# Eight chunks of the first block's modulation: from the tensor engine's row sums to GpSimd products and folds beside the choice of keys

## The chip, the cores and the metric

The kernel runs on one core of a Trainium2 chip. The metric is the device time of one execution in microseconds. Three runs of the kernel before took 4020.67, 4022.31 and 4030.84 us; their median, 4022.31 us, is the time to be compared.

## The reference, cut to what matters

The program computes two transformer blocks one after the other on 1024 tokens of width 1024, all in float32. The part that matters here is the first block's modulation and the choice of keys:

```python
c_act = jax.nn.silu(c)
mod = jnp.matmul(c_act, ada_w[l]) + ada_b[l]          # 1024 -> 6 * 1024
sh1, sc1, gt1, sh2, sc2, gt2 = [m[:, None, :] for m in jnp.split(mod, 6, axis=-1)]
h = rmsnorm(x, norm1_g[l]) * (1.0 + sc1) + sh1
proj = jnp.matmul(h, w_in[l])
...
score = jnp.einsum('bqh,bqhk->bqk', wi[:, start:end].astype(jnp.float32), jax.nn.relu(dots))
_, idx = lax.top_k(score, kk)                          # 256 keys of each query
```

`mod` is one row of 6144 numbers, made in twelve chunks of 512 columns. The first four chunks (sh1, sc1) are needed before anything else; the other eight (gt1, sh2, sc2, gt2) are needed only after the first block's attention.

## The kernel before, in words

The program is written in stages. A stage ends when all five engines have reached its end; then the next one starts. The change lies in one stage, `choose`, which runs from 210.5 to 690.5 us of the profiled execution. Three things run side by side in it.

**The choice of keys.** For the query tiles 2 to 7 (128 queries each; every key is kept for tiles 0 and 1) the scores are made in four pairs of heads per tile, 24 pairs in all. For each pair TensorE makes the products (`ch_s`, L590), ScalarE rectifies them into `ch_relu` (L621), and VectorE adds them, weighted, into `ch_score`: two instructions per pair, the first of a tile at L644 (tensor_scalar), the others at L647 (scalar_tensor_tensor, which reads `ch_relu` and `ch_score`, both in SBUF). I call such a pair of instructions a gather and number them 0 to 23. The choice itself is VectorE's: 32 rounds per tile of the eight largest (L662) and their replacement (L663), and one comparison that writes the mask (L666). After every eighth round of a tile comes one gather for the next tile. So gathers 4 to 23 lie between the rounds of tiles 2 to 6, and tile 7's rounds have none between them.

**The side work of the tensor engine.** A list of tasks (`side_work`) is dealt out to the 24 pairs by a table of costs: 8 small tasks for the logits of the forget gate (`log`), 56 tasks for seven further chunks of `w_in` times eight token tiles (`column`, L564, eight matmuls each), and 8 tasks for the modulation (`vector`). What is left after the last pair comes at the end. ScalarE copies each result out (L610), and for `log` and `column` its queue stores it (L612). ScalarE takes the rectifying and the copies in the order of the list, as TensorE does. TensorE may be two results ahead of the copies. ScalarE rectifies pair u only when gather u-2 is done (`used`).

**A vector task** takes 512 columns of `ada_w`, loaded as [128, 8, 512]. `row_sums` (L100) multiplies each of the eight slices with a broadcast column of silu(c) on a quarter of the array, which leaves four partial rows. ScalarE copies them to `ch_row` (L604). One task later `turn` calls `row_columns` (L108): four matmuls against `pick`, a vector with ones in the four rows that count, which sum the partial rows and turn them into a column of four blocks in `ch_mod`. VectorE adds the bias (L669) as its last instruction of the stage.

SyncE loads two chunks of `w_in` (into `aT`) and one of `ada_w` (into `space`) in the stage before, and then each next one when the last task that reads the buffer is done (`side_done`), in the order of the list.

```python
while left and time > 0:
    time -= cost[left[0][0]]
    share.append(left.pop(0))
```

Of the kernel before, what the change touches and what calls it, by code (L numbers as in the profile page):

```python
# [460 lines left out]
def side_work():  # L461
# [11 lines left out]
    tasks += [("vector", n, None) for n in range(sum(k == "vector" for k, _, _ in tasks), len(vectors))]  # L473
    tasks = logs + tasks
    cost = {"log": 1.6, "column": 6.9, "vector": 4.3}
# [30 lines left out]
def choose(nc, g, iqT, ikT, mask, hT, wi, space, aT):  # L506
# [3 lines left out]
    with stage(nc, g) as ctx:  # L510
# [10 lines left out]
        row = [sb(f"row{b}", [P, CH]) for b in range(2)]  # L521
        mod_ps = ctx.enter_context(nc.psum_tensor("ch_mod", [P, CH], F32))
# [4 lines left out]
        turned = g.sem("ch_turned")  # L527
# [3 lines left out]
        rows_before = [sum(k == "vector" for k, _, _ in tasks[:i]) for i in range(len(tasks) + 1)]  # L531
        outs_before = [sum(k != "vector" for k, _, _ in tasks[:i]) for i in range(len(tasks) + 1)]
# [4 lines left out]
        def _(sp):  # L537
            sp.dma_start(w_log[:, :, :], g.d["w_in"][0].rearrange("(k p) n -> p k n", p=P)[:, :, C_FLOG:C_FLOG + H]).then_inc(log_loaded, 16)
            for i, (kind, n, t) in enumerate(tasks):
                if kind == "column" and t == NT - 1 and n + 2 < len(columns):  # L540
                    sp.wait_ge(side_done, i + 1)
                    load_columns(nc, g, sp, w, n + 2)
                if kind == "vector" and n + 1 < len(vectors):
                    sp.wait_ge(side_done, i + 1)
                    load_vector(nc, g, sp, w_vector, n + 1)

        @block.tensor
        def _(pe):
            def side(i, kind, n, t):
# [3 lines left out]
                if kind == "vector":  # L553
                    pe.wait_ge(g.vector_loaded, 16 * (n + 1))
                    row_sums(nc, side_ps[i % 2], w_vector, g.cT, 0).then_inc(side_done, 1)
                else:
                    if kind == "log":
                        pe.wait_ge(log_loaded, 16)
                        by, width = w_log, H
                    else:  # L560
                        pe.wait_ge(g.columns_loaded[n % 2], 16 * (n // 2 + 1))
                        by, width = w[n % 2], CH
                    for k in range(KD):
                        last = nc.tensor.matmul(side_ps[i % 2][:, 0:width], hT[:, k, t * P:(t + 1) * P], by[:, k, 0:width], start=k == 0, stop=k == KD - 1)  # L564
                    last.then_inc(side_done, 1)

            def turn(i):

                if tasks[i][0] == "vector":
                    k = rows_before[i]  # L570
                    pe.wait_ge(side_copied, i + 1)
                    row_columns(nc, mod_ps[:, 4 * k:4 * k + 4], row[k % 2], g.pick).then_inc(turned, 1)

            def share(i, tasks):
                for kind, n, tile in tasks:
                    side(i, kind, n, tile)
                    if i >= 1:
                        turn(i - 1)
# [15 lines left out]
            turn(i - 1)  # L594

        @block.scalar
        def _(act):
            def side(i, kind, n, t):
                act.wait_ge(side_done, i + 1)
                if kind == "vector":  # L600
                    k = rows_before[i]
                    if k >= 2:
                        act.wait_ge(turned, k - 1)
                    nc.scalar.copy(row[k % 2][:, :], side_ps[i % 2][:, :]).then_inc(side_copied, 1)  # L604
                else:
                    k = outs_before[i]
                    c, width = (C_FLOG, H) if kind == "log" else (columns[n], CH)
                    if k >= OUTS:
                        act.wait_ge(stored[k % OUTS], 16 * (k // OUTS))
# [2774 lines left out]
```

## Time and profile before

| what | us |
|---|---|
| median of three runs | 4022.31 |
| the profiled execution | 4012.1 |
| its span, first to last instruction | 4009.9 |
| TensorE busy in the span | 3754.8 (94%) |
| VectorE busy | 1635.1 (41%) |
| ScalarE busy | 963.8 (24%) |
| GpSimd busy | 328.6 (8%) |
| the stage `choose` | 210.5 to 690.5 |

The profile shows one execution. It is 10.2 us shorter than the median of the unprofiled runs; the sums of the prediction are made inside the profiled execution and then set on the median. GpSimd has no instruction between 0.5 and 708 us, so none in this stage. The chain that ended last does not reach back to this stage: it starts at 3066 us, and since each stage waits for the one before, what the stage gains or loses should be read from its own end.

### The profile page before, as it was taken

To read this page: it belongs to the slowest core of one execution; us is meant where nothing else is said; L and a number is where in the kernel's file an instruction comes from. 1 tells how busy PE (TensorE), PEld (TensorE's weight loads), DVE (VectorE), ACT (ScalarE), POOL (GpSimd) and SP (SyncE) were. 2 spreads that over 40 slices of the span, in tenths; PEclk is the share of its full clock that TensorE was granted. 3 is DMA by queue.
4 is the path that set the end of the run, shared out by engine and by line. 5 is a ranking of instruction groups with operands and counts; after the bars stand their busy time and mean duration, and the time that the engine had idled before them with its cause. 6 is when DMAs were issued, how large, how long until landed. Compare 5 with 4: busy or idle time off the path is not lost. (4 is left out here: it accounts for less than half of the span.)

```text
span 4009.9 us, 46596 instructions
## 1 busy us (share of the span) xinstructions
PE 3754.8 (94%) x18356; PEld 1983.8 (49%) x18356; DVE 1635.1 (41%) x2790; ACT 963.8 (24%) x2001; POOL 328.6 (8%) x302
## 2 busy tenths in 40 slices
PE   6999999999899599999987999999898999999998
PEld 3554444555454244444444457876654444444443
DVE  2469996655232100000002334555453343343246
ACT  2311111544232112212213312222243311111001
POOL 0000000311210201010111111121000000000000
PEclk8979999999999699999996899999898999999999
DMA  4213231111424799898957212322113111111334
GB/s 170 74 38 116 97 116 55 55 59 38 124 87 170 254 344 336 330 342 329 343 202 278 93 67 81 106 81 85 53 35 111 45 42 42 42 42 45 126 111 154
DMA packets 294780, 533.33 MB, mean 133 GB/s; under 512 B 24708, under 2 KB 103828, under 8 KB 292286
## 3 DMA queue, kind: packets, MB, share of 16 engines
q1 hardware_dynamic: 272574, 472.17, 34.2%
q0 software_dynamic: 12720, 43.76, 2.8%
q10 hardware_dynamic: 9296, 14.75, 1.0%
q8 instruction: 134, 2.20, 0.2%
q14 instruction: 56, 0.46, 0.0%
HBM read 462.77 MB, written 67.85 MB: 132 GB/s over the span
## 5 line engine op out<-in xcount | busy, mean ns | idle before, releaser
L564 PE MATMUL ch_side<-aT,space 128*128 128x512 f32 x896 | 392.5, 596 | 0.0
L1679 DVE TENSOR_SCALAR ex_y<-ex_y,ex_entry 128x1024 f32<-128x1024 f32 x32 | 41.1, 1284 | 635.1 <-PE ex_y L1599 635.1
L564 PEld LDWEIGHTS ch_side<-aT,space 128*128 128x128 f32 x896 | 168.3, 190 | 215.3 <-issue 214.1
L2903 PE MATMUL en_bank<-en_h,en_up 128*128 128x512 f32 x528 | 233.8, 592 | 0.0
L1583 PE MATMUL ex_a<-ex_w,ex_xT 128*128 128x512 f32 x512 | 227.6, 598 | 6.2 <-ACT ex_xT L1650 6.2
L1599 PE MATMUL ex_y<-ex_w,ex_actT 128*128 128x512 f32 x512 | 225.1, 592 | 0.7 <-ACT ex_actT L1662 0.7
L1583 PE MATMUL ex_b<-ex_w,ex_xT 128*128 128x512 f32 x512 | 225.0, 592 | 0.0
L2065 PE MATMUL mx_duo<-mx_chunks,mx_region 128*128 128x512 f32 x384 | 181.1, 627 | 0.0
L662 DVE MAX8 ch_best<-ch_score 128x8 f32<-128x384 f32 (+5 forms) x192 | 171.6, 894 | 6.1
L663 DVE MATCH_REPLACE8 ch_score<-ch_best,ch_score 128x384 f32<-128x384 f32 (+5 forms) x192 | 168.0, 875 | 0.0
L2903 PEld LDWEIGHTS en_bank<-en_h,en_up 128*128 128x128 f32 x528 | 100.2, 190 | 125.8 <-issue 125.8
L1583 PEld LDWEIGHTS ex_a<-ex_w,ex_xT 128*128 128x128 f32 x512 | 98.1, 192 | 129.8 <-issue 129.8
L2903 PE MATMUL en_bank<-en_h,en_mixed_up 128*128 128x512 f32 x352 | 158.2, 592 | 0.0
L2012 PE MATMUL mx_duo<-mx_late 64*64 64x64 f32 (+1 forms) x3632 | 146.0, 226 | 6.7 <-DVE mx_late L2644 5.0
L1650 ACT ACTIVATE ex_xT<-ex_x,modT,ex_gain 128x128 f32<-128x128 f32 x264 | 95.6, 467 | 222.8 <-PE ex_x L1588 222.8
L1599 PEld LDWEIGHTS ex_y<-ex_w,ex_actT 128*128 128x128 f32 x512 | 94.8, 190 | 108.0 <-issue 107.1
L1583 PEld LDWEIGHTS ex_b<-ex_w,ex_xT 128*128 128x128 f32 x512 | 94.9, 190 | 107.6 <-issue 107.6
L2012 PEld LDWEIGHTS mx_duo<-mx_late 64*64 64x64 f32 (+1 forms) x3632 | 121.7, 136 | 34.9 <-issue 30.3
L2067 PE MATMUL mx_duo<-mx_chunks,mx_region 128*128 128x256 f32 x512 | 123.2, 395 | 5.0 <-DMA mx_chunks<-w_in 5.0
L610 ACT COPY ch_out<-ch_side 128x512 f32<-128x512 f32 (+1 forms) x64 | 34.1, 533 | 370.6 <-PE ch_side L564 370.6
L3198 DVE TENSOR_TENSOR en_region<-en_region,en_bank 128x512 f32<-128x512 f32 x88 | 58.4, 684 | 158.3 <-PE en_bank L2903 66.6
L2065 PEld LDWEIGHTS mx_duo<-mx_chunks,mx_region 128*128 128x128 f32 x384 | 75.1, 201 | 93.3 <-issue 91.7
(521 smaller groups left out, 5754.7 us busy)
## 6 DMA issues: line engine op xcount, KB each, us to landing
ex_w<-exp_w SPq DMA_DIRECT2D x96, 2048.0 KB, 13.6
en_up<-w_down SPq DMA_DIRECT2D x132, 256.0 KB, 3.6
mx_x<-proj_padded SPq DMA_DIRECT2D x96, 256.0 KB, 3.5
space<-ada_w SPq DMA_DIRECT2D x8, 2048.0 KB, 8.4
space<-w_ada SPq DMA_DIRECT2D x8, 2048.0 KB, 19.7
aT<-w_in SPq DMA_DIRECT2D x7, 2048.0 KB, 8.7
proj<-ch_out ACTq DMA_DIRECT2D x56, 256.0 KB, 2.0
en_up<-w_gate SPq DMA_DIRECT2D x22, 512.0 KB, 5.0
```

Source lines behind the costliest of these rows:

```text
L564: last = nc.tensor.matmul(side_ps[i % 2][:, 0:width], hT[:, k, t * P:(t + 1) * P], by[:, k, 0:width], start=k == 0, stop=k == KD - 1)
L662: chain(nc.vector.max(best[:, :], sc))
L663: chain(nc.vector.match_replace(sc, best[:, :], sc, CHOSEN))
L1583: last = nc.tensor.matmul(ps[:, :], xT[b][:, k, :], w13[b][:, s, k, :], start=k == 0, stop=k == KD - 1)
L1599: last = nc.tensor.matmul(y_ps[:, c:c + CH], actT[:, k, :], w2[b][:, k, c:c + CH], start=k == 0, stop=k == F // P - 1)
L1650: last = nc.scalar.activation(xT[b][:, k, :], x_ps[:, k, :], ACT.Identity, bias=shift[:, k:k + 1], scale=gain[:, k:k + 1])
L1679: nc.vector.tensor_scalar(y[b][:, :], y_ps[:, :], entry[b][:, 2:3].bitcast(F32), None, ALU.mult).then_inc(y_ready, 1)
L2012: mm = lambda out, a, b, start=True, stop=True: nc.tensor.matmul(out, a, b, start=start, stop=stop)
L2065: last = nc.tensor.matmul(ps[:, :], hT[:, k, t * P:(t + 1) * P], w_qkv[c][:, k, :], start=k == 0, stop=k == KD - 1)
L2067: last = nc.tensor.matmul(ps[:, 0:256], hT[:, k, t * P:(t + 1) * P], w_half[c][:, k, :], start=k == 0, stop=k == KD - 1)
L2903: last = nc.tensor.matmul(to[:, :], a[:, k, :], b[:, k, :], start=k == 0, stop=k == HK - 1)
L3198: TT(C[a][b], C[a][b], up_bank(i, m)[:, :], op).then_inc(joined, 1)
```

## The change

The eight vector tasks leave the list of the tensor engine's side work, and the cost of a column in the table goes from 6.9 to 7.1. GpSimd gets a program in this stage: for each chunk it multiplies the whole [128, 8, 512] by silu(c) in place, and folds it in three additions to one [128, 512] in `ch_row`, each instruction waiting for the one before (`weighed`). The tensor engine keeps the four small matmuls per chunk, now against a vector of 128 ones, since all 128 partitions hold a part of the sum. They stand behind the last of tasks 14, 21, 28, 35, 42, 49, 56 and 63. SyncE loads the next chunk when the third fold of the last one is done, at the same places of its list.

```diff
         for t in range(NT):
             tasks.append(("column", n, t))
-            if len(tasks) % 7 == 4 and vectors[len(tasks) // 7:]:
-                tasks.append(("vector", sum(k == "vector" for k, _, _ in tasks), None))
...
-    cost = {"log": 1.6, "column": 6.9, "vector": 4.3}
+    cost = {"log": 1.6, "column": 7.1}
...
+        turn_behind = {NT + 7 * n + 6: n for n in range(len(vectors))}
...
-                if kind == "vector" and n + 1 < len(vectors):
-                    sp.wait_ge(side_done, i + 1)
-                    load_vector(nc, g, sp, w_vector, n + 1)
+                if i in turn_behind and turn_behind[i] + 1 < len(vectors):
+                    sp.wait_ge(weighed, 4 * (turn_behind[i] + 1))
+                    load_vector(nc, g, sp, w_vector, turn_behind[i] + 1)
...
-                if kind == "vector":
-                    pe.wait_ge(g.vector_loaded, 16 * (n + 1))
-                    row_sums(nc, side_ps[i % 2], w_vector, g.cT, 0).then_inc(side_done, 1)
...
+            def turn(k):
+
+                pe.wait_ge(weighed, 4 * (k + 1))
+                if k == 0:
+                    pe.wait_ge(one_set, 1)
+                row_columns(nc, mod_ps[:, 4 * k:4 * k + 4], row[k % 2], one).then_inc(turned, 1)
...
-                    nc.scalar.copy(row[k % 2][:, :], side_ps[i % 2][:, :]).then_inc(side_copied, 1)
...
+        @block.gpsimd
+        def _(pool):
+            nc.gpsimd.memset(one[:, :], 1.0).then_inc(one_set, 1)
+            for n in range(len(vectors)):
+                pool.wait_ge(g.vector_loaded, 16 * (n + 1))
+                if n >= 2:
+                    pool.wait_ge(turned, n - 1)
+                TT = nc.gpsimd.tensor_tensor
+                TT(w_vector, w_vector, g.cT[:, 0:KD].unsqueeze(2).broadcast_to([P, KD, CH]), ALU.mult).then_inc(weighed, 1)
+                pool.wait_ge(weighed, 4 * n + 1)
+                TT(w_vector[:, 0:4, :], w_vector[:, 0:4, :], w_vector[:, 4:8, :], ALU.add).then_inc(weighed, 1)
+                pool.wait_ge(weighed, 4 * n + 2)
+                TT(w_vector[:, 0:2, :], w_vector[:, 0:2, :], w_vector[:, 2:4, :], ALU.add).then_inc(weighed, 1)
+                pool.wait_ge(weighed, 4 * n + 3)
+                TT(row[n % 2][:, :], w_vector[:, 0, :], w_vector[:, 1, :], ALU.add).then_inc(weighed, 1)
```

The table of costs deals the columns anew. TensorE at pairs 6 to 8 (the first rows with a modulation chunk), before:

```order
L590 MATMUL ch_s<-at_ikT,space 128x512 x2
L100 MATMUL ch_side<-space,cT 32x512 x8
L564 MATMUL ch_side<-aT,space 128x512 x8
L108 MATMUL ch_mod<-pick,ch_row 128x1 x4
L590 MATMUL ch_s<-at_ikT,space 128x512 x2
L564 MATMUL ch_side<-aT,space 128x512 x8
L590 MATMUL ch_s<-at_ikT,space 128x512 x2
```

and now:

```order
L583 MATMUL ch_s<-at_ikT,space 128x512 x2
L557 MATMUL ch_side<-aT,space 128x512 x8
L583 MATMUL ch_s<-at_ikT,space 128x512 x2
L557 MATMUL ch_side<-aT,space 128x512 x16
L108 MATMUL ch_mod<-ch_one,ch_row 128x1 x4
L583 MATMUL ch_s<-at_ikT,space 128x512 x2
```

The row sums (eight matmuls of 32 columns of the array) are gone, the four small matmuls stay, and pair 7 has two columns instead of one. TensorE's last rows of the stage, before:

```order
L564 MATMUL ch_side<-aT,space 128x512 x40
L100 MATMUL ch_side<-space,cT 32x512 x8
L564 MATMUL ch_side<-aT,space 128x512 x8
L108 MATMUL ch_mod<-pick,ch_row 128x1 x4
L564 MATMUL ch_side<-aT,space 128x512 x72
```

and now:

```order
L557 MATMUL ch_side<-aT,space 128x512 x48
L108 MATMUL ch_mod<-ch_one,ch_row 128x1 x4
L557 MATMUL ch_side<-aT,space 128x512 x56
L108 MATMUL ch_mod<-ch_one,ch_row 128x1 x4
```

Behind the last pair stood 15 columns and a row sum of these rows (two of the columns belong to the pair's own share); now there are 13 columns, and the last four small matmuls stand behind the last column. GpSimd has this for every chunk (the third here), with its waits:

```order
L624 TENSOR_TENSOR space<-space,cT 128x4096 [waits ch_turned,vector_loaded]
L626 TENSOR_TENSOR space<-space 128x2048 [waits ch_weighed]
L628 TENSOR_TENSOR space<-space 128x1024 [waits ch_weighed]
L630 TENSOR_TENSOR ch_row<-space 128x512 [waits ch_weighed]
```

and SyncE's queue, which loads for it, has now:

```order
L535 DMA ch_w_log<-w_in 128x8x8
L500 DMA space<-ada_w 128x8x512 [waits ch_weighed]
L494 DMA aT<-w_in 128x8x512 [waits ch_side_done]
L500 DMA space<-ada_w 128x8x512 [waits ch_weighed]
L494 DMA aT<-w_in 128x8x512 [waits ch_side_done]
L500 DMA space<-ada_w 128x8x512 [waits ch_weighed]
```

The first `ada_w` load of the stage waits for no task of TensorE any more, and each later one but the last stands directly behind a load of `w_in` in the same queue.

## Rows read from the trace of the kernel before

**Rows 1.** Busy time by stretch (us, busy us and count of each engine, PEclk, DMA share, GB/s)
```profile
665.00:690.00 25.00, 22.29 (x52) 9.50 (x51) 0.00 (x0) 2.34 (x4) 0.00 (x0) 1.00 0.11 42
```

**Rows 2.** Groups by line, 205 to 692 us, VectorE
```profile
L647 DVE SCALAR_TENSOR_TENSOR ch_score<-ch_relu,at_wi,ch_score 128x384 f32<-128x384 f32 (+5 forms) x42 | 40.0, 951 | 38.2 <-ACT ch_relu L621 22.2 <-issue 12.5 <-DVE ch_score L663 0.7
```

**Rows 3.** Timeline of PE, one row sum and its turn (start us, us, what)
```profile
277.82 1.92 PE L100 MATMUL ch_side<-space,cT 128*32 128x512 f32 x16
...
279.67 7.13 PE L564 MATMUL ch_side<-aT,space 128*128 128x512 f32 x16
...
286.64 0.95 PE L108 MATMUL ch_mod<-pick,ch_row 128*128 128x1 f32 x8
```

**Rows 4.** Timeline, end of the stage and start of the next
```profile
664.79 0.19 DVE L669 TENSOR_TENSOR modT<-ch_mod,biasT 128x32 f32<-128x32 f32 x1
...
687.33 0.58 ACT L610 COPY ch_out<-ch_side 128x512 f32<-128x512 f32 x1 [6.28 <-PE ch_side L564]
...
690.49 0.37 SPq L749 DMA_DIRECT2D space<-proj  x1
```

**Rows 5.** Groups by line and form, GpSimd, whole program
```profile
L778 POOL TENSOR_TENSOR space<-space,ad_q_stat 128x1024 f32<-128x1024 f32 x8 | 14.9, 1899 | 19.1 <-DVE ad_q_stat L1024 19.1
...
L1334 POOL TENSOR_TENSOR space<-space,jn_gate_bias 128x2048 f32<-128x2048 f32 x8 | 36.1, 4509 | 100.3 <-DMA space<-proj 100.3
...
L2459 POOL TENSOR_TENSOR mx_early<-mx_early 128x1024 f32<-128x1024 f32 x8 | 19.2, 2397 | 60.9 <-DMA mx_early<-moe_y 60.9
```

**Rows 6.** One line's instructions: duration ns min/median/max, first and last start
```profile
L1387 DVE TENSOR_TENSOR jn_merged<-space x16: 691/693/5855, 1032.5 to 1242.5; 128x512 f32<-128x512 f32 x16
...
L1384 DVE TENSOR_TENSOR space<-space,jn_bank x16: 675/686/689, 1031.2 to 1241.2; 128x512 f32<-128x512 f32 x16
...
L2588 DVE TENSOR_REDUCE mx_pstat<-mx_psq x16: 685/686/687, 2244.4 to 2810.3; 128x8 f32<-128x512 f32 x16
```

**Rows 7.** Timeline of the joining stage, GpSimd and VectorE
```profile
1084.40 4.51 POOL L1334 TENSOR_TENSOR space<-space,jn_gate_bias 128x2048 f32<-128x2048 f32 x1 [6.85 <-DMA space<-proj]
...
1087.45 2.02 DVE L1387 TENSOR_TENSOR jn_merged<-space 128x512 f32<-128x512 f32 x1
```

**Rows 8.** Timeline of the mixing stage, GpSimd and VectorE
```profile
2534.05 1.49 POOL L2482 TENSOR_TENSOR mx_early<-mx_qkv,mx_tab 128x512 f32<-128x512 f32 x1
...
2534.57 1.52 DVE L2612 TENSOR_TENSOR mx_early<-mx_qkv,mx_tab 128x512 f32<-128x512 f32 x1
...
2535.51 1.49 POOL L2485 TENSOR_TENSOR mx_kd<-mx_qkv,mx_tab 128x512 f32<-128x512 f32 x1
```

**Rows 9.** Timeline of SyncE's queue; DMA issues, 240 to 692 us
```profile
310.96 0.37 SPq L497 DMA_DIRECT2D aT<-w_in  x1
...
space<-ada_w SPq DMA_DIRECT2D x7, 2048.0 KB, 8.0
```

**Rows 10.** Timeline of VectorE, instructions that add scores
```profile
238.90 1.34 DVE L647 SCALAR_TENSOR_TENSOR ch_score<-ch_relu,at_wi,ch_score 128x384 f32<-128x384 f32 x2 [7.17 <-ACT ch_relu L621]
...
263.63 1.61 DVE L647 SCALAR_TENSOR_TENSOR ch_score<-ch_relu,at_wi,ch_score 128x512 f32<-128x512 f32 x2 [1.95 <-issue]
...
278.62 1.60 DVE L647 SCALAR_TENSOR_TENSOR ch_score<-ch_relu,at_wi,ch_score 128x512 f32<-128x512 f32 x2 [3.51 <-issue]
...
378.83 2.14 DVE L647 SCALAR_TENSOR_TENSOR ch_score<-ch_relu,at_wi,ch_score 128x768 f32<-128x768 f32 x2
...
430.81 0.69 DVE L644 TENSOR_SCALAR ch_score<-ch_relu,at_wi 128x896 f32<-128x896 f32 x1
...
451.74 2.40 DVE L647 SCALAR_TENSOR_TENSOR ch_score<-ch_relu,at_wi,ch_score 128x896 f32<-128x896 f32 x2 [2.71 <-issue]
...
489.18 2.41 DVE L647 SCALAR_TENSOR_TENSOR ch_score<-ch_relu,at_wi,ch_score 128x896 f32<-128x896 f32 x2
...
556.85 2.67 DVE L647 SCALAR_TENSOR_TENSOR ch_score<-ch_relu,at_wi,ch_score 128x1024 f32<-128x1024 f32 x2 [4.36 <-issue]
...
577.96 2.67 DVE L647 SCALAR_TENSOR_TENSOR ch_score<-ch_relu,at_wi,ch_score 128x1024 f32<-128x1024 f32 x2
```

More of the change, by code:

```diff
@@ L521, in choose @@
         row = [sb(f"row{b}", [P, CH]) for b in range(2)]
+        one = sb("one", [P, 1])
         mod_ps = ctx.enter_context(nc.psum_tensor("ch_mod", [P, CH], F32))
@@ L526, in choose @@
         stored = [g.sem(f"ch_stored{b}") for b in range(OUTS)]
-        turned = g.sem("ch_turned")
+        weighed, turned, one_set = g.sem("ch_weighed"), g.sem("ch_turned"), g.sem("ch_one_set")
         first = TOPK // P
@@ L552, in side @@
                     pe.wait_ge(side_copied, i - 1)
-                if kind == "vector":
-                    pe.wait_ge(g.vector_loaded, 16 * (n + 1))
-                    row_sums(nc, side_ps[i % 2], w_vector, g.cT, 0).then_inc(side_done, 1)
-                else:
[L557 to L572, printed above, removed]
+                if kind == "log":
+                    pe.wait_ge(log_loaded, 16)
+                    by, width = w_log, H
+                else:
+                    pe.wait_ge(g.columns_loaded[n % 2], 16 * (n // 2 + 1))
+                    by, width = w[n % 2], CH
+                for k in range(KD):
+                    last = nc.tensor.matmul(side_ps[i % 2][:, 0:width], hT[:, k, t * P:(t + 1) * P], by[:, k, 0:width], start=k == 0, stop=k == KD - 1)
+                last.then_inc(side_done, 1)
+            def turn(k):
[3 more added lines that the diff above has]
+                row_columns(nc, mod_ps[:, 4 * k:4 * k + 4], row[k % 2], one).then_inc(turned, 1)
             def share(i, tasks):
@@ L599, in side @@
                 act.wait_ge(side_done, i + 1)
[L600 to L603, printed above, removed]
-                    nc.scalar.copy(row[k % 2][:, :], side_ps[i % 2][:, :]).then_inc(side_copied, 1)
[L605 to L609, printed above, removed]
-                    nc.scalar.copy(out[k % OUTS][:, 0:width], side_ps[i % 2][:, 0:width]).then_inc(side_copied, 1)
-                    act.wait_ge(side_copied, i + 1)
-                    act.dma_start(rows(g.d["proj1"])[:, t, c:c + width], out[k % OUTS][:, 0:width]).then_inc(stored[k % OUTS], 16)
+                c, width = (C_FLOG, H) if kind == "log" else (columns[n], CH)
+                if i >= OUTS:
+                    act.wait_ge(stored[i % OUTS], 16 * (i // OUTS))
+                nc.scalar.copy(out[i % OUTS][:, 0:width], side_ps[i % 2][:, 0:width]).then_inc(side_copied, 1)
+                act.wait_ge(side_copied, i + 1)
+                act.dma_start(rows(g.d["proj1"])[:, t, c:c + width], out[i % OUTS][:, 0:width]).then_inc(stored[i % OUTS], 16)
             i = 0
```

10 lines of the change are left out of this document (3 added, 7 removed).

## The prediction

> **What bounds the stage now.** I read the stage by stretches first, then its last rows, then the groups of VectorE. In the last 25 us TensorE is busy for 22.3 and VectorE has no instruction at all [rows 1]: VectorE adds the bias at 664.79 and is through at 665.0, ScalarE copies the last column at 687.33 and stores it, and the next stage starts at 690.49 [rows 4], 3.2 us after that copy began. So TensorE's side work sets the end, and VectorE has 25 us to spare. The second thing to see is that VectorE's spare time lies at the end only: before it, it waited 12.5 us in four places for scores ("issue" [rows 2]; 1.95, 3.51, 2.71 and 4.36 us [rows 10]). Everything else it did back to back. GpSimd is idle throughout.
>
> **What is removed.** A row sum takes from 277.82 to 279.67, 1.85 us [rows 3]; eight of them are 14.8 us of an engine that is never idle here. The small matmuls (0.95 us busy at 286.64 [rows 3]) stay, eight times. The last of them now lies behind the last column, beside ScalarE's last copy and its store, and before VectorE's bias: under 1 us + 0.2 against these 3.2 us, so hidden. ScalarE loses eight copies like the one in rows 4 (0.58 us), for which nobody waits. By TensorE alone the stage ends 14.8 us earlier, at 675.7.
>
> **What is added on GpSimd.** Nearest rows: a product with a broadcast column takes 1.90 us for 1024 elements (L778), an addition 2.40 for 1024 (L2459) and 4.51 for 2048 (L1334) [rows 5]. So the product of 4096 takes 7.6 us (9.0, if it goes like L1334; I take the broadcast's row, as it is the same kind of operand), the folds 4.5, 2.4 and 1.2: 15.7 us per chunk, 126 us in all. Its own time harms nobody: a chunk is turned 60 to 100 us after its load, and a load takes 8.0 us [rows 9]. The Trainium skill, GPSIMD Reference, section 3.1, gives about 2.6 cycles at 1.2 GHz for each element of a two-input operation; that would be an estimated 8.9 us for the product, and some 1.3 us more for each gather that waits it out, 3 to 4 us in all.
>
> **What it does to VectorE.** This is the term that decides. L1387, an addition of two SBUF operands on VectorE, takes 0.69 us, but once 5.86 [rows 6]. At 1087.45 it took 2.02: it ended at 1089.47, and GpSimd's L1334, which began at 1084.40, ended at 1088.91, 0.56 before it [rows 7]. So it stood still until GpSimd's instruction was over. L1384, with one operand in PSUM, never took more than 0.689, and L2588, a reduction with one input, never more than 0.687 [rows 6]. When both engines have several such instructions, they take turns, each waiting for the whole of the other's: GpSimd 1.49, VectorE 1.52, GpSimd 1.49 [rows 8]. L647 reads two SBUF operands. The rounds read one, and no row shows them beside GpSimd; the Trainium skill, SBUF — State Buffer, "Who interferes with whom", states that a one-input VectorE instruction outside its two-port modes does not contend.
>
> A gather that meets a chunk therefore pays twice: the rest of GpSimd's running instruction, and, between its two halves, the whole of GpSimd's next one. I now walk through the chunks. A chunk starts when its load lands. The loads of chunks 2 to 6 stand behind one of `w_in`, issued at 310.96 for the first [rows 9] and now earlier by the row sums ahead of it; two loads of 2 MB take about 14 us (8.0 for one, and the second's 6 at the rate of the first). That gives starts near 323, 385, 447, 508 and 570; chunk 7 follows 24 us behind chunk 6.
> - Chunk 0 (211 to 227) meets gathers that wait for ScalarE anyway (22.2 us [rows 2]): nothing.
> - Chunk 1 (236 to 252), gather 3 at 238.90 [rows 10]: rest 4.5 + next 4.5 = 9.0. The waits 1.95 and 3.51 at gathers 5 and 6 swallow 5.5 of it.
> - Chunk 2 (323 to 339): gather 9 passes just ahead of it, gather 10 meets the second fold: 2.3. If gather 9 is a microsecond later, it pays up to 12 instead.
> - Chunk 3 (385 to 401): gather 13, 378.83 + 5.8 = 384.6: 7.5 + 4.5 = 12.0.
> - Chunk 4 (447 to 463): gather 16, 430.81 + 17.8 = 448.6: 5.0 + 4.5 = 9.5. The wait of 2.71 at gather 17 goes.
> - Chunk 5 (508 to 524): gather 19, 489.18 + 24.6 = 513.8: 2.0 + 4.5, and the mask of tile 5 (L666) behind it meets a fold, 2.0: 8.5. The wait of 4.36 at gather 22 goes.
> - Chunk 6 (570 to 586) lies between gathers 21 and 22: nothing.
> - Chunk 7 (594 to 610): gather 23, 577.96 + 28.7 = 606.7: 2.5.
>
> Sum: 9.0 + 2.3 + 12.0 + 9.5 + 8.5 + 2.5 = 43.8 us, less the 12.5 swallowed: VectorE ends 31.3 later, at 696.3. That is behind TensorE's 675.7, so VectorE now sets the end. The next stage starts some 0.5 us after it, at 696.8 instead of 690.5: **6.3 us later**. The single phases are uncertain, the sum less so: a gather that is caught leaves when the chunk is nearly over, wherever it was caught, so the chunks' times, not VectorE's earlier delays, set where it stands at 463 and 524. TensorE is not held up: gather u-2 is always done before it needs it. Later stages start later by the same amount; nothing in them is changed. On the median: 4022.3 + 6.3 = 4028.6 (the profiled execution: 4018.4).
>
> **Rivals.**
> - *VectorE slips through* (20%). L647 may not stand still as L1387 does, or most gathers miss the chunks. For it: no row shows a scalar_tensor_tensor beside GpSimd, and gathers take only 2 of every 14 to 21 us. Against it: it has the same two operands, and 15.7 us of chunk are as long as a period of gathers. Then TensorE sets the end: ScalarE's copy, 687.33 - 14.8, and the start of the next stage at 675.7: 14.8 us faster, 4007.5. It decides so as long as VectorE loses less than 10.7 + 12.5 = 23 us.
> - *GpSimd takes two turns running* (15%). The 5.86 us of L1387 are more than the 4.51 of any one L1334, so once VectorE waited through more than one instruction [rows 5, 6]. A caught gather would then wait until the chunk is over, up to 15.7 instead of 12.0, and up to 3.7 more at each of five catches: 18.5 us, 4047. If the product also takes 9.0, a few more. Against it: rows 8, and here each of GpSimd's instructions waits for a semaphore of the one before, which leaves VectorE a gap. Slower than before in any case.
> - *The rounds stand still as well* (4%). Seven chunks of 15.7 are 110 us, less 12.5: VectorE ends at 762, 72 us later than the stage's end now, 4094. Against it: L2588.
> - *The forecast* (61%): 2 to 11 us slower, by the product's 7.6 to 9.0 and by gather 9's catch.
>
> **How the numbers follow.** About 0.3%, 12 us, is what a measurement of this kernel can tell from no change. The forecast lies within it; the first rival is faster by more (17% of its 20), the others slower by more (18 of 19%), and 5% of the forecast's own top end goes over. The range reaches from the first rival, 4006, to part of the second, 4037. Faster 0.17, same 0.60, slower 0.23.
>
> **What would show it.** Right: L100 is gone, TensorE ends near 673, and VectorE's bias comes near 696, with a gap on TensorE behind the last column. L647's longest go from 1.3 us to 5 to 8 us, in about ten of its 42, and no "issue" waits remain. GpSimd has 32 instructions near 7.6, 4.5, 2.4 and 1.2 us. L662 and L663 keep their durations (if not, the third rival). Wrong: L647's maximum stays at 1.3, or VectorE ends before 675. The granted clock stays at 1.00 (2.4 GHz) to the last column, as in rows 1; if it fell while TensorE still has columns, the sum would miss a term.

## The result and the profile after

The changed kernel takes 4002.6 us (median of 7 runs, 3996.9 to 4006.5), the kernel before 4020.7 beside it (7 runs): a ratio of 0.9955, with a 95% interval from 0.9939 to 0.9971. That is 18 us faster. The prediction was 6 us slower, in a range from 4006 to 4037. The profiled execution took 3996.9 us (before 4012.1), with a span of 3995.0 us (4009.9).

I read the changed kernel in the order of the prediction. First, who sets the end of the stage: busy time by stretch (columns as in [rows 1]: busy us and count of TensorE, its weight loads, VectorE, ScalarE and GpSimd, the granted clock, the DMA share, GB/s), then the timeline there.

```profile
650.00:675.00 25.00, 23.45 (x61) 10.74 (x59) 23.53 (x30) 2.34 (x4) 0.00 (x0) 1.00 0.11 42
```
```profile
672.50 0.95 PE L108 MATMUL ch_mod<-ch_one,ch_row 128*128 128x1 f32 x8
672.71 0.58 ACT L595 COPY ch_out<-ch_side 128x512 f32<-128x512 f32 x1 [6.28 <-PE ch_side L557]
...
674.04 0.19 DVE L670 TENSOR_TENSOR modT<-ch_mod,biasT 128x32 f32<-128x32 f32 x1
675.88 0.37 SPq L750 DMA_DIRECT2D space<-proj  x1
```

The last 25 us show both engines almost full, where before only TensorE worked [rows 1]. The last column is copied at 672.71 us and the next stage starts 3.17 us later; before it was 687.33 and 3.16 [rows 4]. So TensorE still sets the end, and its end came 14.6 us earlier. The stage itself, from SyncE's first load in it (212.10 us; before 210.52) to the next stage's first, is 463.8 us long in place of 480.0. Below, "the stage" is always this length. VectorE adds the bias 9.3 us later than before (674.04 against 664.79), but that is still early enough: where VectorE ends last (e5_swap, below) the next stage starts 0.67 us after this instruction begins, which would be 674.71 here, 1.2 us before it did. So VectorE had 1.2 us to spare.

Next, GpSimd's groups by line (207 to 677 us), and VectorE's:

```profile
L624 POOL TENSOR_TENSOR space<-space,cT 128x4096 f32<-128x4096 f32 x8 | 56.1, 7015 | 269.8 <-DMA space<-ada_w 269.7
L626 POOL TENSOR_TENSOR space<-space 128x2048 f32<-128x2048 f32 x8 | 36.4, 4549 | 0.6
...
L630 POOL TENSOR_TENSOR ch_row<-space 128x512 f32<-128x512 f32 x8 | 11.8, 1481 | 0.6
```
```profile
L663 DVE MAX8 ch_best<-ch_score 128x8 f32<-128x384 f32 (+5 forms) x192 | 171.6, 894 | 6.1
L664 DVE MATCH_REPLACE8 ch_score<-ch_best,ch_score 128x384 f32<-128x384 f32 (+5 forms) x192 | 168.1, 875 | 0.0
L648 DVE SCALAR_TENSOR_TENSOR ch_score<-ch_relu,at_wi,ch_score 128x384 f32<-128x384 f32 (+5 forms) x42 | 65.2, 1553 | 12.3 <-ACT ch_relu L606 9.1
```

The gathers' 42 instructions take 65.2 us in place of 40.0 [rows 2], and the waits called "issue" are gone. So VectorE was shut out, though less than forecast. The timeline says where. These are all gathers that were caught behind chunk 0, and gather 13 with chunk 3's instructions:

```profile
240.47 9.16 DVE L648 SCALAR_TENSOR_TENSOR ch_score<-ch_relu,at_wi,ch_score 128x384 f32<-128x384 f32 x2 [7.17 <-ACT ch_relu L606]
...
335.90 4.65 DVE L648 SCALAR_TENSOR_TENSOR ch_score<-ch_relu,at_wi,ch_score 128x640 f32<-128x640 f32 x2
...
385.23 2.14 DVE L648 SCALAR_TENSOR_TENSOR ch_score<-ch_relu,at_wi,ch_score 128x768 f32<-128x768 f32 x2
...
401.55 3.12 DVE L648 SCALAR_TENSOR_TENSOR ch_score<-ch_relu,at_wi,ch_score 128x768 f32<-128x768 f32 x2
...
456.27 8.55 DVE L648 SCALAR_TENSOR_TENSOR ch_score<-ch_relu,at_wi,ch_score 128x896 f32<-128x896 f32 x2
...
521.50 2.82 DVE L645 TENSOR_SCALAR ch_score<-ch_relu,at_wi 128x1024 f32<-128x1024 f32 x1
524.42 2.10 DVE L648 SCALAR_TENSOR_TENSOR ch_score<-ch_relu,at_wi,ch_score 128x1024 f32<-128x1024 f32 x1
```
```profile
387.31 7.02 POOL L624 TENSOR_TENSOR space<-space,cT 128x4096 f32<-128x4096 f32 x1 [45.64 <-DMA space<-ada_w]
394.41 4.53 POOL L626 TENSOR_TENSOR space<-space 128x2048 f32<-128x2048 f32 x1
```

Against their undisturbed times (1.34, 1.87, 2.14, 2.40 us, and 0.75 + 1.28) they lose 7.8, 2.8, 1.0, 6.1 and 2.9 us, 20.6 in all; 12.5 of it falls into the "issue" waits of [rows 2]. The line to look at is gather 13. It ended at 387.37 us, and the product that the prediction let it meet began at 387.31: both halves had started before the product did, the second 0.96 us before it, and both kept their length. Gathers 16 and 19, which would have met chunks 4 and 5 after that, started at 438.01 and 499.86 us and were past before these chunks began, at 449.11 and 509.71.

So the prediction's walk and the truth part at one place, chunk 3. Two theories for the runs. **Theory A**: the walk's rules hold, and the place of a few gathers against the chunks, to a microsecond or two, decides between two courses of the stage. **Theory B**: VectorE loses only some 20 us wherever the chunks lie, and the forecast was wrong because its price of a catch was.

### The profile page after: what moved, and what is told of

Its sections match the earlier page's. It is cut to its first block and busy times, and to the rows that moved or that the text cites. A ratio compares the mean times of both kernels' runs of the same rounds, so it can differ in the third digit from the quotient of the medians.

```text
span 3995.0 us, 46360 instructions
## 1 busy us (share of the span) xinstructions
PE 3737.3 (94%) x18228; PEld 1978.0 (50%) x18228; DVE 1669.9 (42%) x2790; ACT 959.2 (24%) x1993; POOL 454.5 (11%) x335
## 5 line engine op out<-in xcount | busy, mean ns | idle before, releaser
L2070 PE MATMUL mx_duo<-mx_region,mx_chunks 128*128 128x512 f32 x256 | 119.2, 620 | 4.5 <-DMA mx_chunks<-w_in 4.5
```

The lines of the kernel that those rows point to most:

```text
L2070: last = nc.tensor.matmul(ps[:, :], w_half[c // 2][:, k, (c % 2) * P:(c % 2 + 1) * P], hT[:, k, t * CH:(t + 1) * CH], start=k == 0, stop=k ...
```

## The experiments

Ratios are against the kernel before, run on the same chip beside it.

| run | median us (runs) | ratio, 95% interval | stage, us |
|---|---|---|---|
| changed kernel | 4002.6 (7) | 0.9955 [0.9939, 0.9971] | 463.8 |
| e1_tiny | 4001.9 (4) | 0.9958 [0.9941, 0.9974] | 464.0 |
| e2_push | 4024.1 (10) | 1.0010 [1.0000, 1.0021] | 485.8 |
| e3_small | 4003.8 (5) | 0.9953 [0.9937, 0.9969] | 464.0 |
| e4_small_push | 3996.7 (4) | 0.9942 [0.9925, 0.9959] | 463.9 |
| e5_swap | 4015.4 (10) | 0.9985 [0.9975, 0.9994] | 480.0 |
| e6_double | 4051.3 (4) | 1.0084 [1.0067, 1.0101] | 514.9 |
| e7_logs_last | 4014.1 (10) | 0.9976 [0.9958, 0.9993] | 478.2 |
| e8_logs_last_small | 3998.4 (5) | 0.9953 [0.9937, 0.9969] | 458.3 |
| e9_spread_small | 3985.4 (4) | 0.9909 [0.9892, 0.9925] | 448.1 |
| e10_push1 | 4001.2 (4) | 0.9942 [0.9921, 0.9963] | 463.8 |
| e11_spread_large | 4007.1 (10) | 0.9972 [0.9961, 0.9983] | 470.2 |
| e12_before_spread | 4005.3 (7) | 0.9969 [0.9957, 0.9980] | 466.2 |

The stage's length is read from one profiled execution of each kernel. It is the sharper figure: the whole time scatters by some 10 us from execution to execution, while the five kernels whose stage TensorE ends in the same order of work (463.8, 464.0, 464.0, 463.9 and 463.8 us) agree within 0.3. How much it varies where VectorE sets the end was not measured.

### GpSimd on four elements

e1_tiny leaves out the weighting and folding of the eight chunks, all but four elements a partition; every instruction, wait and load stays (and GpSimd first sets both `ch_row` buffers to zero).

```diff
-                TT(w_vector, w_vector, g.cT[:, 0:KD].unsqueeze(2).broadcast_to([P, KD, CH]), ALU.mult).then_inc(weighed, 1)
+                TT(w_vector[:, 0, 0:4], w_vector[:, 0, 0:4], g.cT[:, 0:4], ALU.mult).then_inc(weighed, 1)
...
-                TT(row[n % 2][:, :], w_vector[:, 0, :], w_vector[:, 1, :], ALU.add).then_inc(weighed, 1)
+                TT(row[n % 2][:, 0:4], w_vector[:, 0, 0:4], w_vector[:, 1, 0:4], ALU.add).then_inc(weighed, 1)
```

> The changed kernel with GpSimd's four instructions per chunk on four elements each instead of 4096, 2048, 1024 and 512: the products and folds are left out, so eight chunks of the modulation are not computed. Everything else, loads, small matmuls and waits, stays. Theory A (TensorE's path sets the stage's end; what VectorE loses to GpSimd lies inside its slack): the stage is as long as in the changed kernel, 463.8 us within 0.5 (480.0 before); VectorE loses nothing, all weighted additions keep their shortest times, and waits of VectorE for scores come back (about 12 us). The time is that of the changed kernel, 15 to 18 us below the kernel before. Theory B (GpSimd's work costs the changed kernel something on the path): the stage is shorter than 463 us.

VectorE's gathers have their old mean again (951 ns, [rows 2]), and the stage is 464.0 us, the same as with the real work:

```profile
L651 DVE SCALAR_TENSOR_TENSOR ch_score<-ch_relu,at_wi,ch_score 128x384 f32<-128x384 f32 (+5 forms) x42 | 40.0, 951 | 40.6 <-ACT ch_relu L606 22.1 <-issue 15.5
```

So the 25 us that the gathers gained came from GpSimd's elements, and in the changed kernel they cost nothing: this is TensorE's floor.

### Three row maxima ahead of gather 13

The changed kernel, with 2.55 us more for VectorE at one place; their result is overwritten by the next round.

```diff
                     if n % 8 == 7 and t + 1 < NT:
+                        if (t, n) == (4, 15):
+                            for _ in range(3):
+                                chain(nc.vector.max(best[:, :], sc))
                         gather(t + 1, n // 8)
```

> The changed kernel with three further searches for the eight largest (640 wide, 0.83 us each, results overwritten) before VectorE's gather 13, so that this gather starts 2.5 us later, just behind the start of GpSimd's chunk 3 instead of 0.06 us ahead of its end. Theory A (the chain of catches that the prediction walked through is real, and the changed kernel missed it by a hair): gather 13 waits for the product's rest and the next fold, about 11 us; gathers 16, 19 or 20 and 23 are then caught too; VectorE's last instruction comes about 22 us later than in the changed kernel (at 696 instead of 674) and the stage is 485 us long: 5 us slower than before, 21 slower than the changed kernel. Theory B (what GpSimd takes from VectorE hardly depends on the phase, about 20 us either way): VectorE ends 2.5 us later, the stage is about 466 us long, 13 us faster than before.

4024.1 us: 2.55 us of work cost 22.0 us of stage. VectorE's timeline, with GpSimd's third product:

```profile
388.87 7.02 POOL L624 TENSOR_TENSOR space<-space,cT 128x4096 f32<-128x4096 f32 x1 [45.63 <-DMA space<-ada_w]
```
```profile
389.38 12.51 DVE L648 SCALAR_TENSOR_TENSOR ch_score<-ch_relu,at_wi,ch_score 128x768 f32<-128x768 f32 x2
...
451.56 6.53 DVE L645 TENSOR_SCALAR ch_score<-ch_relu,at_wi 128x896 f32<-128x896 f32 x1
458.20 5.21 DVE L648 SCALAR_TENSOR_TENSOR ch_score<-ch_relu,at_wi,ch_score 128x896 f32<-128x896 f32 x1
...
517.17 7.00 DVE L648 SCALAR_TENSOR_TENSOR ch_score<-ch_relu,at_wi,ch_score 128x896 f32<-128x896 f32 x2
524.10 2.70 DVE L670 TENSOR_SCALAR dsa<-ch_score 128x768 f32<-128x768 f32 x1
...
697.86 0.19 DVE L673 TENSOR_TENSOR modT<-ch_mod,biasT 128x32 f32<-128x32 f32 x1
```

Gather 13 is caught and loses 10.4 us. That puts gather 16 into chunk 4 (6.53 and 5.21 us in place of 0.69 and 1.15, 9.9 lost), and gather 19 and the mask of tile 5 into chunk 5 (4.6 + 2.1). This is the prediction's walk, which had 12.0, 9.5 and 8.5, and VectorE's end at 696.3 us. Theory B falls: by it the push would have cost its own 2.55 us, and the stage would have been 466 us long.

### The chunk in fifteen small instructions, without and with the push

```diff
-                TT(w_vector, w_vector, g.cT[:, 0:KD].unsqueeze(2).broadcast_to([P, KD, CH]), ALU.mult).then_inc(weighed, 1)
...
+                part = lambda k: w_vector[:, k, :]
+                for k in range(KD):
+                    TT(part(k), part(k), g.cT[:, k:k + 1].broadcast_to([P, CH]), ALU.mult).then_inc(weighed, 1)
+                done = KD
+                for half in (4, 2, 1):
+                    pool.wait_ge(weighed, 15 * n + done)
+                    for k in range(half):
+                        TT(part(k) if half > 1 else row[n % 2][:, :], part(k), part(k + half), ALU.add).then_inc(weighed, 1)
+                    done += half
```

> The changed kernel with GpSimd's product in eight instructions of 512 elements and the folds in four, two and one of 512, 15 instructions per chunk instead of 4, the same numbers. Theory A (an instruction of VectorE with two SBUF operands waits for one whole instruction of GpSimd at a time, and the engines take turns): a caught gather pays at most 2 x 1.3 us, so no weighted addition is longer than about 3.5 us (8.5 for a pair in the changed kernel); the stage stays at 463.8 us, set by TensorE. Theory B (VectorE waits until GpSimd has no more work): gathers are delayed as in the changed kernel or more, up to 16 us. In both the time is within 3 us of the changed kernel.

> The last two edits together: small GpSimd instructions, and gather 13 pushed 2.5 us behind the start of chunk 3. Theory A (catches cost as much as GpSimd's instruction is long): gather 13 loses 2 us or less, the stage stays at 464 to 466 us, against 485 expected for the push alone. Theory B (the push itself or the number of catches makes the loss, not the length of an instruction): about 485 us.

464.0 and 463.9 us of stage: the push that cost 22 us costs nothing when GpSimd's instructions are short. VectorE's gathers and GpSimd's groups in e3_small:

```profile
L650 DVE SCALAR_TENSOR_TENSOR ch_score<-ch_relu,at_wi,ch_score 128x384 f32<-128x384 f32 (+5 forms) x42 | 49.9, 1189 | 33.0 <-ACT ch_relu L606 20.5 <-issue 8.6 <-DVE ch_score L666 0.9
```
```profile
L626 POOL TENSOR_TENSOR space<-space,cT 128x512 f32<-128x512 f32 x64 | 67.0, 1083 | 256.6 <-DMA space<-ada_w 256.5
L631 POOL TENSOR_TENSOR space<-space 128x512 f32<-128x512 f32 x48 | 66.5, 1414 | 1.3
```

GpSimd is busy longer than before (144 us for the chunks in place of 125), but the gathers take 49.9 us, 15 less: what a gather waits for is the length of one GpSimd instruction, not GpSimd's busy time. The whole times of the two differ by 7 us (their profiled executions by 8) at equal stages, which is scatter elsewhere in the program.

### One row maximum: the edge

The push of e2_push with `range(1)`.

> The changed kernel with one more row maximum (0.83 us) ahead of VectorE's gather 13 instead of three. In the changed kernel's profile gather 13 ended at 387.37 us and chunk 3's product began at 387.31; one push of 0.83 us puts the second instruction's end 0.9 us into the product. Theory A (it is the instruction that starts behind the product's start that is shut out): gather 13's last instruction starts at about 387.1 us, on the edge, so executions fall on one side or the other: times between 4002 and 4024 us, more spread than either kernel alone, median 4002 to 4022 us. Theory B (the push of three cost its time by itself, 2.55 us of 21, in proportion): 4003 to 4009 us.

```profile
386.33 2.14 DVE L648 SCALAR_TENSOR_TENSOR ch_score<-ch_relu,at_wi,ch_score 128x768 f32<-128x768 f32 x2
```

The second half of this gather by itself, and the product:

```profile
387.45 1.02 DVE L648 SCALAR_TENSOR_TENSOR ch_score<-ch_relu,at_wi,ch_score 128x768 f32<-128x768 f32 x1
```
```profile
387.55 7.80 POOL L624 TENSOR_TENSOR space<-space,cT 128x4096 f32<-128x4096 f32 x1 [45.63 <-DMA space<-ada_w]
```

The push did not tip it: 4001.2 us, and no execution came near 4024, so the expected mix of both courses did not show. The reason is in these lines. Gather 13's second half began at 387.45 us, 0.1 before the product, and kept its 1.02 us; this time it was the product that took longer: 7.80 us in place of 7.02. So the instruction that starts first runs to its end, and the other engine's waits. Two outcomes, 0.83 us (this one) and 2.55 us (e2_push) of push, bracket the point of tipping; where between them it lies, and how often an execution of the changed kernel falls over it, stays open. None of its seven runs was longer than 4006.5 us, so it seems that none did.

### The chunks six microseconds earlier

Each load of `ada_w` for chunks 2 to 6 ahead of the load of `w_in` beside it, in SyncE's queue.

```diff
+                if i == NT + 6 or i == NT + 7 * 6 + 6 + 7 * 1:
+                    k = 1 if i == NT + 6 else 7
+                    sp.wait_ge(weighed, 4 * k)
+                    load_vector(nc, g, sp, w_vector, k)
                 if kind == "column" and t == NT - 1 and n + 2 < len(columns):
                     sp.wait_ge(side_done, i + 1)
+                    sp.wait_ge(weighed, 4 * (n + 2))
+                    load_vector(nc, g, sp, w_vector, n + 2)
                     load_columns(nc, g, sp, w, n + 2)
-                if i in turn_behind and turn_behind[i] + 1 < len(vectors):
-                    sp.wait_ge(weighed, 4 * (turn_behind[i] + 1))
-                    load_vector(nc, g, sp, w_vector, turn_behind[i] + 1)
```

> The same GpSimd work as in the changed kernel, but each load of a later chunk stands ahead of the load of the next column in SP's queue, so chunks 2 to 6 start some 6 us earlier (chunk 3 at about 381.5 instead of 387.3 us of the profile), in the middle of VectorE's gathers 13, 16 and 19 instead of just behind them. Theory A (a gather's place against the chunk's start decides): these gathers are shut out as the prediction's walk had it, VectorE sets the end, the stage is 475 to 486 us long from SP's first load of it to its first load of the next stage (463.8 in the changed kernel), the whole 4012 to 4025 us. Theory B (GpSimd's chunks cost VectorE only what the changed kernel's trace shows, wherever they stand; the stage has room): 4000 to 4006 us, stage 464 us.

4015.4 us, stage 480.0. GpSimd does the same work; VectorE's timeline and the next stage's start:

```profile
324.15 10.26 DVE L651 SCALAR_TENSOR_TENSOR ch_score<-ch_relu,at_wi,ch_score 128x640 f32<-128x640 f32 x2
...
393.02 6.18 DVE L651 SCALAR_TENSOR_TENSOR ch_score<-ch_relu,at_wi,ch_score 128x768 f32<-128x768 f32 x2
...
693.38 0.19 DVE L673 TENSOR_TENSOR modT<-ch_mod,biasT 128x32 f32<-128x32 f32 x1
694.05 0.37 SPq L753 DMA_DIRECT2D space<-proj  x1
```

Now chunk 2 catches gather 9, the other near miss that the prediction named, and the rest follows. VectorE sets the end, 0.67 us before the next stage. The order of two loads cost the change's whole gain in this stage.

### A longer chunk

A second product of 4096 elements a partition, by ones, in each chunk; the counts that others wait for go up with it.

```diff
+                pool.wait_ge(weighed, 5 * n + 1)
+                TT(w_vector, w_vector, one[:, 0:1].unsqueeze(2).broadcast_to([P, KD, CH]), ALU.mult).then_inc(weighed, 1)
```

> One more product of 4096 elements a partition in each chunk (by ones, so nothing changes in the values): GpSimd is busy some 7 us longer a chunk, 8 times. Theory A: gathers that passed just ahead of a chunk, and those just behind, are now caught; each that stands behind the whole longer chunk waits up to 22 us instead of 15. VectorE sets the end by a wide margin: stage 490 to 515 us, the whole 4028 to 4055 us, slower than the kernel before. Theory B (room on VectorE): at most the 8 x 7 = 56 us of which 35 are swallowed by idle time, but only if VectorE meets them; the stage stays 464 to 470 us, the whole 4000 to 4010 us.

```profile
L651 DVE SCALAR_TENSOR_TENSOR ch_score<-ch_relu,at_wi,ch_score 128x384 f32<-128x384 f32 (+5 forms) x42 | 124.7, 2969 | 8.1 <-ACT ch_relu L606 3.7 <-issue 1.3
```

4051.3 us, 29 us above the median of the kernel before (4021.9), ratio 1.0084, within both figures of theory A. The gathers take 124.7 us, three times their own 40.0; the rounds keep their 894 and 875 ns here too.

### The log groups: a second cost of TensorE

While reading who sets the end, one row stood out. In both kernels TensorE works at the lower clock level (granted 0.50, 1.2 GHz) as long as the eight log groups last, though it is hardly idle there, and it is at 1.00 (2.4 GHz) once the columns run. Busy time by stretch, the changed kernel:

```profile
212.00:249.00 37.00, 36.34 (x149) 30.39 (x150) 25.57 (x12) 4.93 (x17) 27.11 (x7) 0.50 0.20 59
249.00:672.00 423.00, 423.00 (x1091) 187.16 (x1092) 407.07 (x627) 62.30 (x95) 97.76 (x27) 1.00 0.24 89
```

The log groups have eight columns per matmul. I put them last, with large and with small GpSimd instructions:

```diff
-    tasks = logs + tasks
+    tasks = tasks + logs
...
-        turn_behind = {NT + 7 * n + 6: n for n in range(len(vectors))}
+        turn_behind = {7 * n + 6: n for n in range(len(vectors))}
```

> The eight small groups for the log columns, which open the stage at half clock (3.48 us each), stand at its end instead. Theory A: TensorE does them in 1.8 us each, and the scores' first matmuls come sooner for VectorE: TensorE's end comes 8 to 14 us earlier (stage 450 to 456 us), but the gathers stand elsewhere against the chunks, so with large GpSimd instructions VectorE sets the end anywhere from 452 to 480 us: the whole 3990 to 4018 us. Theory B (clock stays low until it has run for its time, whichever matmuls stand there): no gain, 4000 to 4006 us with the granted clock still 0.5 over the first 35 us, columns then at 11 to 13 us instead of 6.9.

> The same, with GpSimd's chunk in 15 instructions of 512 elements, which shut VectorE out for at most 1.4 us at a time. Theory A: VectorE gets through whatever the places; TensorE sets the end; if the clock is up 8 to 14 us are saved, 3988 to 3996 us, stage 450 to 456 us. Theory B (clock stays low whichever matmuls stand there): 4000 to 4006 us, stage 462 to 466 us.

e8_logs_last_small has a stage of 458.3 us, 5.7 less than e3_small: between what the two theories expected, and no measurable gain in the whole. Its last columns and the logs behind them:

```profile
647.36 23.18 PE L557 MATMUL ch_side<-ch_w_log,space 128*128 128x8 f32 x128
```
```profile
645.00:650.00 5.00, 5.00 (x36) 4.04 (x35) 4.86 (x7) 0.75 (x2) 0.00 (x0) 1.00 0.14 52
650.00:655.00 5.00, 5.00 (x34) 5.00 (x34) 4.90 (x5) 0.33 (x2) 0.00 (x0) 0.71 0.07 7
655.00:660.00 5.00, 5.00 (x25) 5.00 (x25) 4.72 (x8) 0.17 (x1) 0.00 (x0) 0.50 0.02 1
```

The clock was 1.00, TensorE went from columns to logs with no gap, and it fell during them. So the clock fell while a row of log groups ran, with no idle time ahead of it. e7_logs_last shows the same: its logs begin at 645.19 us, and the clock is 1.00 from 640 to 645 and 0.50 from 650 to 655. e7_logs_last had VectorE as its bound again (stage 478.2); its ten runs reach from 3991 to 4020 us, with two below 3997. Whether those two missed the chunks isn't known, as no trace of them was taken.

If the row of logs is the cause, they should cost half when they stand alone among columns (e9_spread_small, with GpSimd's fifteen small instructions; the list of the columns behind which a turn stands follows the new order):

```diff
             tasks.append(("column", n, t))
-    tasks = logs + tasks
+            if len(tasks) % 8 == 4:
+                tasks.append(logs[len(tasks) // 8])
```

> GpSimd's chunk in 15 instructions, and the eight small log groups neither first nor last but one behind about every seventh column group. With the logs last the granted clock was 1.00 over the columns from 230 us on and fell to 0.50 some 5 us into the logs (640 to 675 us), without idle time ahead of it, and the stage got only 5.6 us shorter. Theory A (the run of log groups itself, back to back, takes the clock down): each alone among columns runs at full clock, 1.75 us in place of 3.49, 14 us saved and 1 to 2 more on the scores beside them: stage 447 to 451 us (464.0 with the logs first), the whole 3984 to 3992 us. Theory B (the clock falls for another reason at the start and at the end of the stage): stage 455 to 462 us, the whole 3992 to 4002 us.

3985.4 us, stage 448.1. One log group, the stage's clock and its end:

```profile
247.54 1.95 PE L559 MATMUL ch_side<-ch_w_log,space 128*128 128x8 f32 x16
```
```profile
212.00:650.00 438.00, 435.70 (x1226) 200.10 (x1223) 404.57 (x629) 67.19 (x111) 140.62 (x121) 1.00 0.25 90
```
```profile
656.38 0.59 ACT L597 COPY ch_out<-ch_side 128x512 f32<-128x512 f32 x1 [6.28 <-PE ch_side L559]
...
657.28 0.19 DVE L674 TENSOR_TENSOR modT<-ch_mod,biasT 128x32 f32<-128x32 f32 x1
659.55 0.37 SPq L754 DMA_DIRECT2D space<-proj  x1
```

A log group takes 1.95 us in place of 3.5 (28.0 us for eight), and the clock is 1.00 throughout. This is the fastest of all kernels here: 35 us under the one before, where the change gained 18. TensorE and VectorE now end within a microsecond of each other.

Two more tell whether the parts add up: the spread logs with the changed kernel's large instructions, and in the kernel before.

> The log groups spread, with GpSimd's chunk in the changed kernel's four large instructions (e9_spread_small had 15 small ones: stage 448.1 us, 3985.4 us). Theory A (large instructions shut VectorE's gathers out, and TensorE's end now lies 16 us earlier, so that VectorE's slack of 1 us is gone): VectorE sets the end, stage 458 to 480 us, the whole 3995 to 4018 us, over 9 us slower than with small ones. Theory B (in this order of the work the gathers happen to miss the chunks again): 3984 to 3992 us.

> The kernel before, with nothing but its eight log groups spread (one behind every eight other tasks). Theory A (the logs' half clock is a cost of its own, beside GpSimd's chunks): 16 us less, as from e3_small to e9_spread_small: stage 463 to 467 us in place of 480.0, the whole 4002 to 4008 us, so that the change's 15 us and the logs' 16 us add up. Theory B (the log groups cost more only beside GpSimd's work): 4015 to 4022 us.

```diff
-    tasks = logs + tasks
+    for k in range(NT):
+        tasks.insert(9 * k + 4, logs[k])
```

e12_before_spread: 4005.3 us, stage 466.2, 13.8 less than 480.0. The median gained 12 us and the stage 13.8, where 16 were expected: the logs' cost is one of its own, nearly as large as the row sums' 14.8. With small GpSimd instructions the two parts add up to within 2 us: 480.0 less 448.1 is 31.9 us, against 16.2 + 13.8. Where some of the missing 2 us went is in the trace of e12_before_spread, at the one place where a row sum, a log group and a turn stand in a row:

```profile
299.87 1.92 PE L100 MATMUL ch_side<-space,cT 128*32 128x512 f32 x16
301.73 1.95 PE L565 MATMUL ch_side<-ch_w_log,space 128*128 128x8 f32 x16
303.53 1.26 PE L108 MATMUL ch_mod<-pick,ch_row 128*128 128x1 f32 x8
```
```profile
304.00:308.00 4.00, 4.00 (x11) 2.21 (x11) 3.79 (x7) 0.00 (x0) 0.00 (x0) 0.57 1.04 394
```

The clock fell behind them as well, from 1.00 to a mean of 0.57 over 4 us, though TensorE was busy throughout; from 308 us on it was 1.00 again. The column matmuls of this stage take 391.3 us, from each start to the next, 1.4 more than in the kernel before.

e11_spread_large: 4007.1 us, stage 470.2, 22 us longer than with small instructions. Its instructions with two operands in SBUF, and the first ones of a tile:

```profile
L650 DVE SCALAR_TENSOR_TENSOR ch_score<-ch_relu,at_wi,ch_score 128x384 f32<-128x384 f32 (+5 forms) x42 | 70.4, 1676 | 5.2 <-ACT ch_relu L608 1.9
L647 DVE TENSOR_SCALAR ch_score<-ch_relu,at_wi 128x384 f32<-128x384 f32 (+5 forms) x6 | 19.2, 3206 | 1.5 <-ACT ch_relu L608 1.3
```

VectorE lost more here than in the changed kernel (70.4 + 19.2 us, there 65.2 + 11.8), and the slack that made its losses free there is used up: the last column is copied at 657.25 us, and the bias comes at 680.16. So with large instructions the parts do not add up.

## Why the prediction was wrong

- **What is removed: right, 1.4 us short.** Eight row sums, 14.8 us. TensorE's end came 14.6 us earlier on the clock of the profile, but that this agrees to 0.2 is chance: the stage began 1.6 us later in this execution, and got shorter by 16.2. Counted from each matmul's start to the next one's, the row sums were 14.8 us. The last turn, 0.8 us of TensorE's time, now stands behind the last column (672.50 us); the prediction called it hidden and did not subtract it. The other 0.6 us lie in the column matmuls (389.35 us in place of 389.90), and why is not shown.
- **What GpSimd takes: nearly right.** The folds 4.5 us as forecast. The product took 7.0 us, not 7.6: 0.6 off. By the Trainium skill, GPSIMD Engine Reference, section 3.1, it would be an estimated 8.9; the trace decides for 7.0.
- **How a catch works: right.** A gather that starts behind a GpSimd instruction is shut out for the rest of it, and its second half for nearly the whole of the next (4.06 us beside a fold of 4.53). Gather 3 lost 7.8 us (forecast 9.0), gather 10 lost 2.8 (2.3), and in e2_push gathers 13, 16 and 19 with the mask lost 10.4, 9.9 and 6.7 (12.0, 9.5, 8.5). That the mask counts was luck: the walk had 2.0 us for it, in e2_push it lost 2.15, but the prediction gave its reason only for instructions of two operands in SBUF. The stage there was 485.8 us long, 2.55 of it the push itself; the forecast's, 696.8 less 210.5, was 486.3. The rounds kept their durations, so the third rival fell, and the second as well: no gather waited through two of GpSimd's instructions in one of its own halves (the longest in e2_push was 7.3 us, its own 1.0 included, beside a product of 7.0).
- **The step that failed: "Chunk 3 (385 to 401): gather 13, 378.83 + 5.8 = 384.6: 7.5 + 4.5 = 12.0."** This is an overlap that did not take place. The prediction itself put gather 13 at 384.6 and the chunk at 385, 0.4 us apart, with two guesses in the first (the catches at chunks 1 and 2) and one in the second (14 us for two loads). Measured from the stage's start, the gather came 1.0 us earlier than said (385.23 - 1.6 = 383.6) and the chunk 0.7 later (387.31 - 1.6 = 385.7). Even on the prediction's own numbers the first half would have passed, and only the second, at 385.7, would have been caught, for an estimated 6.9 us (to the product's end at 392.6). Gather 16 would then have stood at 443.5 and been over by 445.5, ahead of chunk 4 at 447. The catch did not take place, and with it went those of gathers 16 and 19; what came at chunks 3, 4 and 5 in their place were 1.0, 6.1 and 2.9 us, at gathers 14, 17 and 20, and nothing in place of the 2.5 at chunk 7. VectorE lost 20.6 us instead of 43.8, below the 23 that the prediction named as the first rival's point of decision. So the first rival came true by its second reason, that gathers miss the chunks; its first, that they may not stand still at all, is refuted.
- **The sentence behind it: "The single phases are uncertain, the sum less so".** It is true of gathers that are caught, and only of them. In e2_push and e5_swap each catch put a gather into the next chunk, and in the changed kernel the miss put gathers 16 and 19 ahead of it, so 2.55 us at one gather moved the stage by 22. VectorE's bias came 461.9 us behind the stage's start in the changed kernel, and 479.3 (e5_swap) and 485.1 (e2_push, 2.55 of it the push). A walk that hung on 0.4 us had no ground for 61% on its own result and 20% on the other.
- **The range** ended at 4006, and the measured 4002.6 lies below it. The first rival, which came true, had 4007.5: 14.8 us under 4022.3. The seven runs of before beside the changed kernel had 4020.7, and the interval of the ratio allows a gain of 12 to 25 us; the range had left no room for either.

## What to carry to other kernels

When a long GpSimd instruction is put beside VectorE work of two SBUF operands, the cost can depend on where they meet, to a microsecond or two, as it did here; a walk that decides on such a margin gives two forecasts, and both deserve a chance near one half. Cutting the GpSimd work into pieces costs GpSimd some busy time (here 15%) and took the luck out at the one place that was tried: the same push cost 22 us beside four large instructions and nothing beside fifteen small ones. And when an engine that is never idle sets the end, read its granted clock by stretch before counting its instructions: a row of very narrow matmuls was here nearly as dear as all the work that the change removed (13.8 us of stage against 14.8).

## What the runs showed of the hardware

- GpSimd and VectorE shut each other out by the instruction, first come, first served, in both directions: gather 13 waited for a product and a fold in e2_push (12.51 us in place of 2.14), and in e10_push1 a product that began 0.1 us behind the gather's second half took 7.80 us instead of 7.02.
- Not only instructions of two SBUF operands are shut out. The first of a tile's gathers, a tensor_scalar with one large operand (`ch_relu`) and a column, took 6.65 us in place of 0.42 at chunk 0, and the comparison that writes the mask 2.70 us in place of 0.55 (e2_push). The row maxima and replacements never were, in 192 of each (means 894 and 875 ns in both kernels). The Trainium skill, SBUF — State Buffer, "Who interferes with whom", states that one-input VectorE instructions outside its two-port modes do not contend; the rounds agree. The tensor_scalar stands on the other side of that line, and its own speed in the kernel before goes with that: 0.42 us for 384 elements a partition and 0.75 for 1024 are 0.52 ns for each further element, half of the 1.04 ns of the scalar_tensor_tensor (0.62 and 1.28 us) and of the 1.06 ns of the row maxima (0.55 and 1.23).
- The granted clock fell from 1.00 to 0.50 while TensorE was busy without a gap, in matmuls of eight columns, where its weight loads filled the time (5.00 us of 5.00). Single groups of them among columns left it at 1.00 in e9_spread_small and e11_spread_large, and in e12_before_spread all but the one that stood between a row sum and a turn. At the stage's start something else takes part as well: from 206 to 212 us, before any log, it was already 0.75 in the changed kernel (TensorE busy for 3.05 us of the 6), and 1.00 in e9_spread_small (2.90 of 6). What decides there stays open; with columns behind that gap the clock was 1.00 again from 222 us on (e7_logs_last, e8_logs_last_small), with logs it stayed at 0.50 for 37 us. So some of e9_spread_small's shorter stage may be luck: e11_spread_large has the same order of work on TensorE, was at 0.50 from 207.5 to 214 us, and copied its last column 446.6 us after the stage's start, where e9_spread_small needed 444.9.
